# Interleaving the two k rows of each stationary weight half, so that TensorE reads its stationary tiles with a step of 8 bytes

## What is computed

```python
shift, scale, gate = split(c @ w_mod + b_mod, 3)
u = x * (1 + scale) + shift
q, k, v, z_a, cb, cc, cx, z_b, g_a, g_b = split(u @ w_in)        # 2048 -> 12288
y_a = rmsnorm(diff_attention(rope(q), rope(k), v)) * gain * silu(z_a)   # 8 heads
y_b = cb * causal_conv3(cc * cx) * silu(z_b)
h   = sigmoid(g_a) * (y_a @ w_proj_a) + sigmoid(g_b) * (y_b @ w_proj_b)
out = layernorm(alpha * x + gate * (h @ w_out)) * ln_gain + ln_bias
```

## Time and profile before

| | |
|---|---|
| time, median of 3 runs | 1563.55 us (1563.29 to 1564.33) |
| time of the profiled execution | 1565.23 us |
| its span, first to last instruction | 1563.5 us |
| matmul engine busy (PE) | 1498.8 us, 96% |
| weight loads (PEld) | 1220.2 us, 78% |
| VectorE (DVE) | 819.4 us, 52% |
| ScalarE (ACT) | 501.1 us, 32% |
| granted TensorE clock, mean | 0.991 of full speed |

### The profile page before, as it was taken

One profiled execution on the slowest core, in us unless ns is written; L12 is line 12 of the kernel. 1 busy time (PEld: TensorE's weight loads), 2 busy tenths in 40 slices (PEclk: granted clock), 3 DMA queues, 4 the chain that ended last, 5 costly groups with the idle time before them and its releaser, 6 DMA issues.

```text
span 1563.5 us, 18079 instructions
## 1 busy us (share of the span) xinstructions
PE 1498.8 (96%) x6600; PEld 1220.2 (78%) x6600; DVE 819.4 (52%) x1072; ACT 501.1 (32%) x693; POOL 44.0 (3%) x52
## 2 busy tenths in 40 slices
PE   2889999999999999999999999999999999999994
PEld 2667788787887878878787888888788888888883
DVE  6997764647546375463754742222522323434448
ACT  1215434425344243443434422223122221422121
POOL 0000000000000000000000000000000000000004
PEclk9999999999999999999999999999999999999997
DMA  9995432533324334233433232322232232362312
GB/s 346 382 382 155 135 108 69 147 107 107 108 85 130 107 111 123 82 114 107 132 110 94 82 135 80 107 93 96 82 107 98 90 107 80 108 254 96 107 54 108
DMA packets 215248, 200.22 MB, mean 128 GB/s; under 512 B 7729, under 2 KB 176433, under 8 KB 214449
## 3 DMA queue, kind: packets, MB, share of 16 engines
q1 hardware_dynamic: 209648, 176.52, 34.9%
q0 software_dynamic: 4608, 16.78, 3.9%
q10 hardware_dynamic: 962, 6.53, 1.0%
HBM read 195.61 MB, written 4.19 MB: 128 GB/s over the span
## 4 chain that ended last, share of the span: by engine, by line
PE 88%; DVE 7%; issue 2%; ACT 1%; DMA 1%; SPq 0%; POOLq 0%; POOL 0%; ACTq 0%; DVEq 0%
PE acc L992 28%; PE acc L993 28%; PE acc L994 28%; DVE mod_sum L631 2%; PE sc L1081 2%; DVE w_lo L604 1%; PE misc L1099 1%; DMA w_mod_in<-in_w_mod 1%; PE sc L1090 1%; DVE res L975 1%; DVE res L951 0%; ACT act_hi L431 0%; DVE gate L653 0%; PE misc L1041 0%; DVE act_lo L658 0%
## 5 line engine op out<-in xcount | busy, mean ns | idle before, releaser
L604 DVE TENSOR_TENSOR w_lo<-raw,w_hi 128x1024 fp32r<-128x1024 f32 (+1 forms) x258 | 310.6, 1215 | 599.6 <-ACT w_hi L388 599.5
L992 PE MATMUL acc<-act_hi,w_hi 128*128 128x512 f32 x1472 | 579.2, 394 | 21.8 <-DVE w_lo L604 13.9
L994 PE MATMUL acc<-act_hi,w_lo 128*128 128x512 f32 x1472 | 574.8, 390 | 0.0
L993 PE MATMUL acc<-act_lo,w_hi 128*128 128x512 f32 x1472 | 574.3, 390 | 0.0
L388 ACT ACTIVATE w_hi<-raw 128x1024 fp32r<-128x1024 f32 (+1 forms) x258 | 268.9, 1052 | 720.0 <-PE acc L994 637.9
L992 PEld LDWEIGHTS acc<-act_hi,w_hi 128*128 128x128 f32 x1472 | 277.2, 188 | 93.6 <-issue 35.8
L994 PEld LDWEIGHTS acc<-act_hi,w_lo 128*128 128x128 f32 x1472 | 277.3, 188 | 58.6
L993 PEld LDWEIGHTS acc<-act_lo,w_hi 128*128 128x128 f32 x1472 | 277.5, 189 | 56.7 <-issue 0.2
L994 PE MATMUL acc<-y_hi,w_lo 128*128 128x512 f32 x256 | 99.6, 389 | 0.0
L992 PE MATMUL acc<-y_hi,w_hi 128*128 128x512 f32 x256 | 99.6, 389 | 0.0
L993 PE MATMUL acc<-y_lo,w_hi 128*128 128x512 f32 x256 | 99.6, 389 | 0.0
(11 more groups left out here) (151 smaller groups left out, 990.9 us busy)
## 6 DMA issues: line engine op xcount, KB each, us to landing
raw<-in_w_in SPq DMA_DIRECT2D x256, 256.0 KB
w_mod_in<-in_w_mod SPq DMA_DIRECT2D x64, 512.0 KB, 6.9
raw<-in_w_tail SPq DMA_DIRECT2D x32, 1024.0 KB
raw<-in_w_in SPq DMA_DIRECT2D x29, 1024.0 KB
gate_in<-in_w_mod POOLq DMA_DIRECT2D x32, 512.0 KB, 4.2
x_in<-in_xT SPq DMA_DIRECT2D x8, 512.0 KB, 8.0
x_tok<-in_x ACTq DMA_DIRECT2D x1, 4096.0 KB, 13.2
raw<-in_w_in SPq DMA_DIRECT2D x8, 384.0 KB
```

The costliest lines, as they stand in the source:

```text
L604: ins = dve.tensor_tensor(w_lo[:, f % SLOTS, :, 0:width], raw[:, (f // 2) % 2, 2 * (f % 2):2 * (f % 2) + 2, 0:width], w_hi[:, f % SLOTS, : ...
L992: pe.matmul(dst, a_hi, b_hi, start=first, stop=False)
L993: pe.matmul(dst, a_hi, b_lo, start=False, stop=False)
L994: return pe.matmul(dst, a_lo, b_hi, start=False, stop=last)
```

## The change

The halves from `HEAD0` on are stored differently where the weights are stationary. Before, a slot holds the 512 columns of row 0 and behind them the 512 of row 1. After, the two rows are interleaved element by element: column m of row kk stands at element 2m + kk. A stationary tile of 128 columns is then read with a step of two elements, 8 bytes, over 1024 bytes. ScalarE writes `w_hi` in that order, VectorE reads `w_hi` and writes `w_lo` in it. `raw` stays as it was. `h` is stored likewise in `act_hi` and `act_lo`, in pairs of k rows, for the output product, where it is stationary; there the weights move and stay plain. Halves below `HEAD0`, and every moving operand, stay plain. No instruction is added or removed, and no wait.

```diff
+        def in_pairs(rows):
+            return rows.rearrange("p k c -> p (k c)").rearrange("p (m k) -> p k m", k=2)
+        def h_rows(tile, k):
+            return in_pairs(tile[:, k - k % 2:k - k % 2 + 2, :])[:, k % 2]
...
-            def round_raw(f, i, per):
+            def round_raw(f, i, per, plain):
...
-                copy(w_hi[:, f % SLOTS, :, 0:width],
-                     raw[:, unit % 2, 2 * (f % 2):2 * (f % 2) + 2, 0:width]).then_inc(hi_ready, 1)
+                rows = raw[:, unit % 2, 2 * (f % 2):2 * (f % 2) + 2, 0:width]
+                if plain:
+                    copy(w_hi[:, f % SLOTS, :, 0:width], rows).then_inc(hi_ready, 1)
+                else:
+                    copy(in_pairs(w_hi[:, f % SLOTS]), rows).then_inc(hi_ready, 1)
...
-                            copy(act_hi[:, k, :], h[:, k, :]).then_inc(h_hi_ready, 1)
+                            copy(h_rows(act_hi, k), h[:, k, :]).then_inc(h_hi_ready, 1)
...
+                else:
+                    ins = dve.tensor_tensor(in_pairs(w_lo[:, f % SLOTS]), rows,
+                                            in_pairs(w_hi[:, f % SLOTS]).bitcast(F32), ALU.subtract)
...
-                dve.tensor_tensor(act_lo[:, k, :], h[:, k, :], act_hi[:, k, :].bitcast(F32), ALU.subtract
-                                  ).then_inc(h_split, 1)
+                dve.tensor_tensor(h_rows(act_lo, k), h[:, k, :],
+                                  h_rows(act_hi, k).bitcast(F32), ALU.subtract).then_inc(h_split, 1)
...
-                            ins = three(acc[:, n, :], m_hi[:, k, cols], m_lo[:, k, cols],
+                            ins = three(acc[:, n, :], h_rows(m_hi, k)[:, cols], h_rows(m_lo, k)[:, cols],
                                         w_hi[:, slot, kk, :], w_lo[:, slot, kk, :], *ends)
+                        elif first + s < HEAD0:
+                            ins = three(acc[:, n, :], w_hi[:, slot, kk, cols], w_lo[:, slot, kk, cols],
+                                        m_hi[:, k, :], m_lo[:, k, :], *ends)
                         else:
-                            ins = three(acc[:, n, :], w_hi[:, slot, kk, cols], w_lo[:, slot, kk, cols],
+                            ins = three(acc[:, n, :], in_pairs(w_hi[:, slot])[:, kk, cols],
+                                        in_pairs(w_lo[:, slot])[:, kk, cols],
                                         m_hi[:, k, :], m_lo[:, k, :], *ends)
```

More of the change, by code:

```diff
@@ L394, in round_raw, with round_at @@
                 width = G_TILES * P if f < 2 * GROUPS and f % 2 else COLS
-                copy(w_hi[:, f % SLOTS, :, 0:width],
-                     raw[:, unit % 2, 2 * (f % 2):2 * (f % 2) + 2, 0:width]).then_inc(hi_ready, 1)
-            def round_at(first, i, per, s):
+                rows = raw[:, unit % 2, 2 * (f % 2):2 * (f % 2) + 2, 0:width]
[3 more added lines that the diff above has]
+                    copy(in_pairs(w_hi[:, f % SLOTS]), rows).then_inc(hi_ready, 1)
+            def round_at(first, i, per, s, plain=None):
                 act.wait_ge(half_done, i * per + (first + s - LEAD + BASE))
-                round_raw(first + s, i, per)
+                round_raw(first + s, i, per, first + s < HEAD0 if plain is None else plain)
             def drain_head(i, z_done):
@@ L435, in _ @@
                     if f < SLOTS:
-                        round_raw(f, 0, 0)
+                        round_raw(f, 0, 0, True)
                     else:
@@ L536, in merge_b @@
                 for s in range(MERGE_HALVES):
-                    round_at(B0, i, MERGE_HALVES, s + LEAD)
+                    round_at(B0, i, MERGE_HALVES, s + LEAD, last and s + LEAD >= MERGE_HALVES)
                     if s == 7:
@@ L566, in _ @@
                 for s in range(OUT_HALVES):
-                    round_at(O0, i, OUT_HALVES, s + LEAD)
+                    round_at(O0, i, OUT_HALVES, s + LEAD, True)
             for s in range(OUT_HALVES - LEAD):
-                round_at(O0, D // COLS - 1, OUT_HALVES, s + LEAD)
+                round_at(O0, D // COLS - 1, OUT_HALVES, s + LEAD, True)
             for t in range(NT):
@@ L597, in close, with lo_half @@
                 count[1] = 0
-            def lo_half(first, i, per, s):
+            def lo_half(first, i, per, s, plain=None):
                 dve.wait_ge(hi_ready, i * per + (first + s + 1))
@@ L603, in lo_half @@
                 width = G_TILES * P if f < 2 * GROUPS and f % 2 else COLS
-                ins = dve.tensor_tensor(w_lo[:, f % SLOTS, :, 0:width],
-                                        raw[:, (f // 2) % 2, 2 * (f % 2):2 * (f % 2) + 2, 0:width],
-                                        w_hi[:, f % SLOTS, :, 0:width].bitcast(F32), ALU.subtract)
+                rows = raw[:, (f // 2) % 2, 2 * (f % 2):2 * (f % 2) + 2, 0:width]
+                if f < HEAD0 if plain is None else plain:
+                    ins = dve.tensor_tensor(w_lo[:, f % SLOTS, :, 0:width], rows,
+                                            w_hi[:, f % SLOTS, :, 0:width].bitcast(F32), ALU.subtract)
+                else:
+                    ins = dve.tensor_tensor(in_pairs(w_lo[:, f % SLOTS]), rows,
+                                            in_pairs(w_hi[:, f % SLOTS]).bitcast(F32), ALU.subtract)
                 ins.then_inc(lo_ready, 1)
@@ L906, in h_lo @@
                 dve.wait_ge(h_hi_ready, k + 1)
-                dve.tensor_tensor(act_lo[:, k, :], h[:, k, :], act_hi[:, k, :].bitcast(F32), ALU.subtract
-                                  ).then_inc(h_split, 1)
+                dve.tensor_tensor(h_rows(act_lo, k), h[:, k, :],
+                                  h_rows(act_hi, k).bitcast(F32), ALU.subtract).then_inc(h_split, 1)
             def merge_b(i, last=False):
                 for s in range(MERGE_HALVES):
-                    lo_half(B0, i, MERGE_HALVES, s + LEAD)
+                    lo_half(B0, i, MERGE_HALVES, s + LEAD, last and s + LEAD >= MERGE_HALVES)
                     if last and s > 7:
@@ L959, in _ @@
                 for s in range(OUT_HALVES):
-                    lo_half(O0, i, OUT_HALVES, s + LEAD)
+                    lo_half(O0, i, OUT_HALVES, s + LEAD, True)
                 residual(i, range(NT), i * OUT_STEPS)
@@ L964, in _ @@
             for s in range(OUT_HALVES - LEAD):
-                lo_half(O0, last, OUT_HALVES, s + LEAD)
+                lo_half(O0, last, OUT_HALVES, s + LEAD, True)
             for t in range(NT):
@@ L1151, in _ @@
                         cols = slice(t * P, (t + 1) * P)
-                        ins = three(acc[:, t, :], act_hi[:, k, cols], act_lo[:, k, cols],
+                        ins = three(acc[:, t, :], h_rows(act_hi, k)[:, cols], h_rows(act_lo, k)[:, cols],
                                     w_hi[:, (O0 + s) % SLOTS, kk, :], w_lo[:, (O0 + s) % SLOTS, kk, :],
```

## The result

The changed kernel takes 1606.1 us (median of 4 runs, 1605.52 to 1606.27) against 1563.67 (4 runs, 1563.29 to 1564.33): slower by the ratio 1.027, 95% interval 1.0252 to 1.0288. The prediction said 1502. The profiled execution took 1606.05 us around a span of 1604.4, 40.9 us more than the 1563.5 of before.

What follows compares the result with a forecast made beforehand. The prediction took the distance between TensorE's matmul starts as the bound. From 1563.5 us it took 65 for faster matmuls and added 3 for waits in the heads: 1501.5, put as 1502, range 1489 to 1590.

Steps and rivals of the forecast that it cites:

- What bounds the kernel, and the one number it hangs on: From about 165 to 1542 us the distance between matmul starts on TensorE, 0.2267 us, sets the end.
- The distance, its excess, and that the moving stream and the load both have a part in it: Each full-clock fp32r matmul costs 0.0133 us over its columns, from weight load and moving stream meeting in memory.
- The step that failed: Stepped weight loads in 5760 matmuls would advance as fast as the moving stream, so the excess goes.
- 65 us less: 5760 matmuls with stepped stationary tiles each lose 0.0113 us, giving a distance of 0.2154 us.
- Rival 3: A stepped load costs TensorE more: twice the places touched, excess doubled, 1640 us; chance 0.16.
- VectorE's subtraction at no extra price: Subtractions of 240 halves with stepped operands cost nothing more; upper bound 1.08 us each.
- ScalarE's rounding at no extra price: Roundings of 240 halves written stepped cost nothing more; upper bound 0.92 us each.
- Waits in the heads: Faster TensorE would wait 0.3 us a head, 1 us more in the first: 3 us more together.
- The range: 1489 to 1590 us, said to leave out under 0.2 of the chances.
- rival 2: The excess is fixed, matmuls stay at 0.2267 us: 1563.5 with free writes (0.11), up to 1606 with slow writes (0.11).

Runs made afterwards that it cites:

- move_one_place: Kernel before, with the moving operand of every fp32r weight product one element read 512 times (another product): 1504.88 us.
- load_step8: Kernel before with plain stores, stationary tiles read with a step of two elements wherever the changed kernel does (another product): 1605.59 us, ratio 1.0265.
- move_back_step8: Kernel before with the fp32r moving operand read back to front and stationary tiles read at a step of 8 bytes from plain stores: 1601.58 us.
- move_twice: Kernel before with a moving operand of 256 elements read twice each, advancing over memory at half speed (another product): 1506.25 us.
- after_break: Changed kernel with one float32 transpose of 128 columns into an idle PSUM bank ahead of the merges: 1602.83 us.
- columns256: Kernel before with each fp32r matmul cut into two of 256 columns, so twice the weight loads, same product: 1639.3 us.
- move_hop: Kernel before with moving columns taken in turn from the operand's two halves, 4 elements each, and written to PSUM in that order, same product: 1699.66 us.

## Why the prediction was wrong

- *What bounds the kernel, and the one number it hangs on*: right. The distances of starts grew by more than the 40.9 us of span, and the start and the tail gave 1.4 back.
- *The distance, its excess, and that the moving stream and the load both have a part in it*: right, and now shown by move_one_place and load_step8. So was the price of it: without it the kernel takes 1504.88 us against the 1502 that I forecast for such a case, and the only new wait of TensorE there is 1.0 us at the scores.
- *The step that failed*: "With a step of 8 bytes the load advances over 1024 bytes in the time in which it advanced over 512, as fast as the fp32r moving stream", and the choice from it that the excess goes. The term was "65 us less", at a distance of 0.2154; the measured distance is 0.2333 or 0.2356, an excess of 0.0200 or 0.0222 in place of 0.0020, and the term is some 42 us more. I read the disappearance at the low clock and with float32 as a matter of equal speeds. move_back_step8 and load_step8 have equal speeds and keep the excess; move_twice loses it when the moving stream goes at half pace, with the load left as it was. The simpler reading, that at half pace the moving stream has room for a load, fits both; whether it has room for a stepped load too was not run. Why the step of 8 bytes raises the excess at full pace is argued only: it breaks every aligned pair of a load (theory G2). Both readings fitted the rows before; I chose the one that needed a coincidence.
- *Rival 3* had the direction and the mechanism ("the moving stream is disturbed by loads"), at 0.16. Its size, a doubled excess and 1640, was off: the excess grew by half. 5760 x 0.0067 = 38.4 us, and about 4 more, less the 1.4 of start and tail: the 40.9. The 4 go with the slower rhythm in the first merges (960 matmuls) and in 240 matmuls in a row of each of the first seven heads; by the count it would cost 2640 x 0.0022 = 5.9, and the rest of that is not accounted for.
- *VectorE's subtraction at no extra price*: right, 1224 ns. The Trainium skill, "Vector Engine (DVE) Microarchitecture Reference", section 5.2, says that a VectorE port keeps its full rate only on runs of at least two adjacent words from an 8-byte boundary. The trace does not agree for a step of 8 bytes in this instruction, on one source and the destination: 1224 ns stepped, 1223 plain. *ScalarE's rounding at no extra price*: 0.07 us a rounding too low, and hidden. The count in the prediction, 240, was too high: the weights of the output product stay plain, and 208 are stepped.
- *Waits in the heads*: none came, since TensorE got slower and its slack grew. The range, up to 1590, missed 1606.1 by 16 us; it cut off the two cases that went higher, most of rival 3 (0.16) and the end of rival 2. That rival 2 with slow writes names 1606 is chance: its excess stays at 0.0133 and its 42 us are waits for slow writes in and before the heads, and the profile has neither that excess nor those waits.

None of the versions that compute the same product beats the kernel before: after_break 1602.83, columns256 1639.3, move_hop 1699.66.

## What to carry to other kernels

In this kernel's stream of fp32r matmuls, each with a tile of its own, every matmul and its load cost 0.0133 us over the columns at the full clock when the tile is 128 adjacent elements on an 8-byte boundary, and about half as much again when it is stepped or one word off. Keep stationary tiles contiguous and aligned, and read the distance of starts, not durations, to see what a change did. When an excess is gone in two cases, ask first what those cases have in common that is simplest, here spare pace of one stream, and test the disputed read alone before moving the stores.

## What was not expected of the hardware

- A stream kept one rhythm for over 200 us and 960 matmuls, with 235.56 or 233.33 ns on average for identical reads; one float32 transpose switched it (after_break).
- With a load of one element 128 times the starts are further apart (0.2311 in the earlier window, 0.2317 in the later) than with 128 adjacent elements (0.2267).
- Weight loads are listed hardly longer at a step of 8 bytes and much longer at 12 and 16: 0.195, 0.251 and 0.306 us each, against 0.188 for adjacent elements.
- Still open: why reading the moving operand back to front costs 0.0067 a matmul with adjacent tiles and nothing more with stepped ones.
